# A two-block transformer-like layer at sequence 256: the residual and most products turned from feature-major to token-major

## The reference, cut to what matters

```python
x: (1, 256, 2048) float32                      # T = 256 tokens, D = 2048 features
h    = rmsnorm(x, norm_mix_pre)
proj = h @ w_in                                # 2048 x 5120: pool input, q, f, i, g
mix  = concat(pool_mixer(...), hgrn2_mixer(...)) @ w_out
x    = x + rmsnorm(mix, norm_mix_post)
h    = rmsnorm(x, norm_mlp_pre)
x    = x + rmsnorm(square(relu(h @ w_mlp_in)) @ w_mlp_out, norm_mlp_post)   # 8192 hidden
m    = silu(c) @ ada_w + ada_b                 # six vectors of 2048, one row c
n    = rmsnorm(x, norm_g[0]) * (1 + m[1]) + m[0]
z    = gelu(n @ a_w_in); u, v = split(z)       # 4096 each
s    = w_s . rmsnorm(v) (+ b_s)                # mixing over tokens in chunks of 128
x    = x + m[2] * ((u * s) @ a_w_out)
n    = rmsnorm(x, norm_g[1]) * (1 + m[4]) + m[3]
z    = conv3 along tokens of (n @ ffn_w_up); g, v = split(z)                # 5632 each
x    = x + m[5] * ((silu(g) * v) @ ffn_w_down)
out  = rmsnorm(x, final_g)
```

## Time and profile before

| | us |
|---|---|
| median of 3 runs (range) | 2573.86 (2572.02 to 2575.58) |
| span of the profiled execution | 2572.2 |
| PE busy in it | 2494.5 (97%) |
| DVE busy | 1682.6 (65%) |
| ACT busy | 1154.8 (45%) |

### The profile page before, as it was taken

One profiled execution on the slowest core, in us unless ns is written; L12 is line 12 of the kernel. 1 busy time (PEld: TensorE's weight loads), 2 busy tenths in 40 slices (PEclk: granted clock), 3 DMA queues, 4 the chain that ended last, 5 costly groups with the idle time before them and its releaser, 6 DMA issues.

```text
span 2572.2 us, 50625 instructions
## 1 busy us (share of the span) xinstructions
PE 2494.5 (97%) x19544; PEld 2437.4 (95%) x19544; DVE 1682.6 (65%) x1941; ACT 1154.8 (45%) x1344; POOL 100.1 (4%) x71
## 2 busy tenths in 40 slices
PE   8999998999999999998999999998999999999998
PEld 7989997999999999997888999998999999999997
DVE  6784767776675765776866876655666556655665
ACT  5554544543543543543544533434544344443443
POOL 0330011000000000001000000000000000000000
PEclk9999998999999999998999999999999999999999
DMA  6434453776777776774787776454555555555553
GB/s 224 140 132 164 141 194 109 299 274 253 260 278 254 257 278 251 257 273 168 262 312 259 271 279 237 158 187 151 184 180 174 194 173 181 182 184 180 187 181 123
DMA packets 151486, 542.88 MB, mean 211 GB/s; under 512 B 17712, under 2 KB 20016, under 8 KB 151216
## 3 DMA queue, kind: packets, MB, share of 16 engines
q1 hardware_dynamic: 151344, 540.81, 59.8%
HBM read 538.64 MB, written 2.10 MB: 210 GB/s over the span
## 4 chain that ended last, share of the span: by engine, by line
PE 92%; DVE 4%; issue 2%; ACT 1%; DMA 1%; POOL 0%; DVEq 0%; SPq 0%; ACTq 0%
PE bank L340 28%; PE bank L341 27%; PE bank L342 27%; PE bank L356 2%; PE bank L357 2%; PE bank L358 2%; PE mis L420 1%; DVE acc L1022 1%; DMA raw<-wstream 1%; DVE wlo L969 1%; PE mis L524 1%; DVE rstd L1015 0%; PE bank L377 0%; PE mis L401 0%; ACT whi L575 0%
## 5 line engine op out<-in xcount | busy, mean ns | idle before, releaser
L969 DVE TENSOR_TENSOR wlo<-raw,whi 128x1024 fp32r<-128x1024 f32 x824 | 1011.1, 1236 | 717.2 <-ACT whi L575 712.7
L575 ACT ACTIVATE whi<-raw 128x1024 fp32r<-128x1024 f32 x824 | 861.3, 1056 | 1093.8 <-PE bank L342 794.2
L340 PE MATMUL bank<-xs,whi 128*128 128x256 f32 x3456 | 986.9, 286 | 33.1 <-issue 13.1
L341 PE MATMUL bank<-xs,whi 128*128 128x256 f32 x3456 | 983.4, 285 | 0.0
L342 PE MATMUL bank<-xs,wlo 128*128 128x256 f32 x3456 | 983.3, 285 | 0.0
L340 PE MATMUL bank<-hs,whi 128*128 128x256 f32 x2496 | 707.8, 284 | 0.0
L341 PE MATMUL bank<-hs,whi 128*128 128x256 f32 x2496 | 706.3, 283 | 0.0
L342 PE MATMUL bank<-hs,wlo 128*128 128x256 f32 x2496 | 706.3, 283 | 0.0
L340 PEld LDWEIGHTS bank<-xs,whi 128*128 128x128 f32 x3456 | 669.4, 194 | 36.0 <-issue 28.7
L341 PEld LDWEIGHTS bank<-xs,whi 128*128 128x128 f32 x3456 | 669.4, 194 | 0.3 <-issue 0.2
L342 PEld LDWEIGHTS bank<-xs,wlo 128*128 128x128 f32 x3456 | 669.0, 194 | 0.0
(11 more groups left out here) (153 smaller groups left out, 1058.9 us busy)
## 6 DMA issues: line engine op xcount, KB each, us to landing
raw<-wstream SPq DMA_DIRECT2D x824, 512.0 KB, 4.4
aring<-astream SPq DMA_DIRECT2D x192, 512.0 KB, 4.6
x<-xT SPq DMA_DIRECT2D x4, 512.0 KB, 5.6
outT<-acc SPq DMA_DIRECT2D x4, 512.0 KB, 2.7
pw<-poolw SPq DMA_DIRECT2D x1, 1024.0 KB, 9.2
ws<-wsT SPq DMA_DIRECT2D x8, 128.0 KB, 4.2
bs<-bsp SPq DMA_DIRECT2D x8, 128.0 KB, 4.6
mk<-masks SPq DMA_DIRECT2D x1, 288.0 KB, 8.5
```

The costliest lines, as they stand in the source:

```text
L340: pe.matmul(o, whi[:, slot, c], h, start=st, stop=False, skip_group_check=True)
L341: pe.matmul(o, whi[:, slot, c], l, start=False, stop=False, skip_group_check=True)
L575: act.activation(whi[:, slot, :], raw[:, slot, :], ACT.Copy).then_inc(hi_ready, 1)
L969: dve.tensor_tensor(wlo[:, slot, :], raw[:, slot, :], whi[:, slot, :].bitcast(F32), ALU.subtract).then_inc(lo_ready, 1)
```

## The change

The residual `x`, the accumulator `acc` and the outputs of most products become token-major (tokens on partitions). `token_unit` is now used for groups 4, 5, 8 to 69 and for all down groups of the feed-forward; `feature_unit` stays in groups 0 to 3, 6, 7 and in the feed-forward's up groups, where the convolution runs along tokens. Sums of squares run along the free axis, as an accumulated output of ACT's Square, so a norm's scale is one number to a partition. What a product takes as its stationary operand still needs features on partitions: PE transposes each 128x128 tile through the identity (`to_features` for a sublayer's input, eight steps of four transposes, three before its first unit and five between its units; `hidden_to_features` for a group of hidden activations, eight transposes between units of the next group; `heads_to_features` for the mixer). ACT and DVE make high and low parts from the transposed tiles in PSUM. Gains that multiply columns of a token-major tile are loaded as rows broadcast to all partitions, 1 MB each. Two of the six modulation vectors are now reduced by matmuls with a matrix of ones (`ada_row`), so that they come out broadcast. All `Fori` loops are written out.

```diff
@@ TensorE @@
+            def token_unit(src, kt0, n, first, last, pb):
+                pe.wait_ge(lo_ready, n + 1)
+                slot = n % RING
+                for k in range(UK):
+                    c = slice(k * NC, (k + 1) * NC)
+                    for b in range(2):
+                        o = bank[pb + b][:, :]
+                        h = src[:, kt0 + k, b * P:(b + 1) * P]
+                        l = src[:, kt0 + k, T + b * P:T + (b + 1) * P]
+                        pe.matmul(o, h, whi[:, slot, c], start=first and k == 0, stop=False)
...
+            def to_features(z, i):
+
+                pe.wait_ge(xn_ready, 8 * z + i + 1)
+                if i >= 4:
+                    pe.wait_ge(tm_ready, 8 * z + i - 3)
+                for k in range(2):
+                    for b in range(2):
+                        o = mis[i % 4][:, k * T + b * P:k * T + (b + 1) * P]
...
+            def hidden_to_features(hg, pair):
+                pe.wait_ge(tok_ready, hg + 1)
+                for m in range(MT):
+                    for b in range(2):
+                        mm = pe.transpose(mis[pair + m // 2][:, (m % 2) * T + b * P:(m % 2) * T + (b + 1) * P],
+                                          t1[:, b, m * P:(m + 1) * P], eye[:, :])
...
+            def ada_row(v):
+                pe.wait_ge(ada_used, (v + 1) * ADA_PER_VEC)
+                for c in range(4):
+                    mm = pe.matmul(mis[c][:, :], ones[:, :], aacc[:, c * NC:(c + 1) * NC], start=True, stop=True)
+                mm.then_inc(ada_sum, 2)
...
-            with pe.Fori(0, 4) as q:
-                with pe.Fori(0, 2) as p:
-                    for a in range(2):
-                        group(q * 8 + p * 2 + (G_MLP + a), xs, 2 * a, wait=xs0(1))
...
+            for q in range(4):
+                for p in range(4):
+                    j, hg = G_MLP + 8 * q + p, 4 * q + p
...
+            pe.wait_ge(ws_arrived, 16 * 8)
+            pe.wait_ge(ada_read, 5)
@@ ScalarE @@
+            def feature_tmp(z, i):
+                act.wait_ge(xt_done, 8 * z + i + 1)
...
+            def features(z, j, first=None):
+
+                feature_tmp(z, 0)
+                for i in range(8):
+                    if i < 7:
+                        feature_tmp(z, i + 1)
+                    act.wait_ge(tm_ready, 8 * z + i + 1)
+                    act.activation(xs[:, 2 * i:2 * i + 2, 0:T], tiles(t1[:, i % 2, :]), ACT.Copy).then_inc(xs_hi, 1)
...
+                def evac(j=j):
+                    if j >= 8:
+                        act.wait_ge(h_ff, 2)
+                        act.wait_ge(unit_used, evac_at(j))
+                        for b in range(2):
+                            act.activation(sgt[:, b, (j - 8) * NC:(j - 7) * NC], bank[2 * (j % 2) + b][:, :],
+                                           ACT.Sigmoid).then_inc(bank_free, 1)
@@ VectorE @@
+            def gate_take(v, gate, r):
+                dve.wait_ge(row_arrived[r], 16)
+                dve.wait_ge(ada_sum, 2 * v + 2)
+                for c in range(4):
+                    o = gate[:, c * NC:(c + 1) * NC]
+                    ins = dve.tensor_tensor(o, mis[c][:, :], o, ALU.add)
+                ins.then_inc(ada_read, 1)
...
+            def joined(i):
+                if i % 2 == 0:
+                    normed_sum(S_MIX, i * T, NC).then_inc(xn_ready, 2)
...
+            for g in range(8):
+                body(G_AV + g, None, after=(lambda i: gate_take(4, gate2, ROW_GATE) if i == 7 else None) if g == 7 else None,
+                     done=RING if g == 0 else 0)
```

More of the change, by code:

```diff
@@ L272, in ada @@
                     sp.wait_ge(ada_used, k - 1)
[L273 to L282, removed]
+                sp.dma_start(aring[:, k % 2, :], astream[k:k + 1, :, :].rearrange("o p w -> p (o w)")
+                             ).then_inc(ada_arrived[k % 2], 16)
@@ L359, in token_unit, with group @@
                 mm.then_inc(unit_used, 1)
[L361 to L365, removed]
+            def group(j, src, token=True, wait=None, between=None):
+                n, units = first_unit(j), units_of(j)
+                if j >= 2:
+                    pe.wait_ge(bank_free, 2 * j - 2)
@@ new lines, in _, with between @@
+                for g in range(4):
+                    def between(u, g=g):
+                        if g == 0 and u == 2:
+                            pe.wait_ge(hid_lo, 2 * (H_A + 4 * half + 3))
+                            hidden_to_features(H_A + 4 * half + 3, 2)
+                        if half == 0 and g == 3 and u == 6:
+                            ada_row(5)
+                    group(G_AU + 8 * half + 4 + g, hs, wait=lambda u: (hid_lo, 2 * (H_A + 4 * half) + u + 1),
+                          between=between)
@@ L561, in _ @@
+            enter(3)
+            for c in range(3):
+                ups = 8 if c < 2 else 6
+                for p in range(ups):
+                    group(G_FF + 12 * c + p, xs, token=False, wait=normed(3),
+                          between=entering(3) if c == 0 and p == 0 else None)
+                for g in range(4):
+                    group(G_FF + 12 * c + ups + g, hs, wait=lambda u: (hid_lo, 2 * (H_F + 4 * c) + u + 1))
         @block.scalar
         def _(act):
-            step = Count(act_step)
+            steps, cells, squares = [0], [0], [0]
@@ L575, in split, with body @@
                 act.activation(whi[:, slot, :], raw[:, slot, :], ACT.Copy).then_inc(hi_ready, 1)
[L577 to L580 removed]
+            def body(j, evac, after=None, done=0, last=True):
+                units = units_of(j)
                 for i in range(units):
[L582 removed]
+                    if i == units - 1 and evac:
@@ L837, in _ @@
-            mlp_quarter(0, early=True)
-            with act.Fori(1, 3) as q, step.loop(q, 2, 8, start=1):
-                mlp_quarter(q)
-            mlp_quarter(3, last=True)
-            root(3)
-            squares(4, x, ready=lambda i: sum_ready(1, i))
-            root(4)
-            split_xs(2, shift=mod[:, 0, :], meanwhile=early_splits(G_AV))
-            def gated_values(p, early=False):
-                for a in range(2):
-                    j = p * 2 + (G_AV + a)
-                    body(j * GU, lambda: gelu_v(j, p * 2 + a, a), done=0 if a or not early else EARLY)
@@ L1354, in _ @@
-            mlp_quarter(0, early=True)
-            ada_take(0)
-            with dve.Fori(1, 3) as q, step.loop(q, 2, 1, start=1):
-                mlp_quarter(q)
-                ada_take(q)
-            mlp_quarter(3)
-            dve.wait_ge(ada_read, 3)
-            link(dve.scalar_tensor_tensor(out=geff[:, :], in0=mod[:, 1, :], scalar=1.0, in1=gain[:, 4, :],
-                                          op0=ALU.add, op1=ALU.mult))
-            root(3)
-            normed_into_x(1, 3)
-            root(4)
@@ L1428, in _ @@
-            ffn_chunk(0, early=True)
-            ffn_chunk(1)
-            with dve.Fori(0, 3) as p, step.loop(p, 3, 4):
-                j = p * 2 + G_FT
-                body(j * GU, lambda: gate(j, 0, p + 8), late=True)
-                body((j + 1) * GU, lambda: value(j + 1, 1, p + 8, p + (H_F + 8), p * 4), late=True)
-            for g in range(4):
-                n = G_DT * GU + g * DTU
-                body(n, lambda: gated_into_x(n + DTU, g % 2, 4 * g, 5), units=DTU, s0=2 * (g % 2))
-            root(6)
```

1540 lines of the change are left out of this document (816 added, 724 removed).

## The result

| | median us | range | to the kernel before |
|---|---|---|---|
| before, timed beside it (4 runs) | 2574.15 | 2572.02 to 2575.58 | |
| after (4 runs) | 3398.55 | 3397.41 to 3401.96 | 1.3203 [1.3184, 1.3222] |

What follows compares the result with a forecast made beforehand. The prediction took PE, dense inside groups, as the bound, so the number and width of its instructions count. Its terms summed to -87.7 us, span 2572.2 to 2484.5, giving a median of 2486 us, range 2464 to 2513.

Steps and rivals of the forecast that it cites:

- DMA: Loads of the 1 MB gain rows, one as groups 46 and 47 start: between 0 and 6 us, 3.5 taken.
- Modulation: Reducing modulation vectors: two by `ada_row` matmuls, +3.5 us, and 1 us where `ada_columns` waits for the last tile.
- DMA becomes the bound: Rival: weight supply stays at its old pace in the MLP's 32 groups, 41 us given back, 2527 us; chance 0.08.
- Products: 520 units become token-major with half as many matmuls, 2.72 us a unit instead of 2.88: -83.2 us.
- Transposes: 0.85 us per eight in 24 MLP and chunk-mixer groups, +20.4 us; twenty at each of four entries, +8.6 us.
- Loops: Writing out loops removes PE's stops at three quarter turns and, at half, one of the feed-forward's chunks: -21.3 us.
- slower than before: Rival: reading the written-out program costs stops everywhere, 0.85 us in each of 104 groups using up the gain; chance 0.03.
- Boundaries: PE's stops: mixer to MLP 8.6 us (-17.2), MLP to chunk mixer 18 (-8), chunk mixer to feed-forward 9.2 (-0.6).
- New wait before group 54: PE stands while DVE reads the reduced vector behind group 53's last split, low clock after: +8.7 us, bounds 3 and 12.
- The start: Kernel start: first product at 17.2 us instead of 20.7, -3.5 us.
- The gains' row: 1 MB rows of gains, one asked for as groups 46 and 47 start: 3.5 us taken for all.
- Mixer's end and the kernel's end: Mixer's end, groups 8 to 10, head norms replaced and late splits: net +3.3 us; kernel's end 12.8 us for 15.7: -2.9.

Runs made afterwards that it cites:

- experiment 1: The changed kernel with SyncE asking for each modulation tile k where the kernel before did, instead of tile k+2 there: 2489.77 us, ratio 0.9665.
- experiment 6: Experiment 1 with each transpose of the hidden activations issued twice: 2510.21 us, ratio 0.9753.
- experiment 3: The kernel before with its loops written out and nothing else changed: 2551.32 us, ratio 0.9909.
- experiment 8: Experiment 7 with the fourth weight split placed behind the norm's root at the MLP's end, on ACT and DVE: 2474.57 us, ratio 0.9614.
- experiment 2: Experiment 1 with DVE reading the gate's vector ahead of the last weight split of group 53: 2478.58 us, ratio 0.9631.
- experiment 7: Experiment 2 with the gate's row and first part of the v gain asked for four groups later: 2478.11 us, ratio 0.9630.

## Why the prediction was wrong

**The step that failed** is in the parts "DMA" and "Modulation": the first prices only the gains' rows, the second only the reduction by `ada_row` and `ada_columns`. That the requests of the 192 modulation tiles stand at other places in SyncE's queue was left out, and with it a term of +909 us (experiment 1 against after). The account of the change shows lines of PE, ACT and DVE and none of SyncE, where this one stands. No rival held it: "DMA becomes the bound" is a want of bandwidth, and names "ACT waiting for DMA with PE waiting for it" as its sign. That sign did appear, 1428 us of it, with the DMA engines at 0.42. The same wait row can mean a full pipe or an empty one; the share beside it decides.

The price could have been worked out from the trace before: 4.4 us from request to landing, ACT 1.06 and DVE 1.24 and 1.28, 0.4 for the tile's request ahead of the unit's: 8.4 us in all, for a unit that PE needs every 2.72. These two lines of the page before were the missing ones (queue, count, size, us to landing):

```profile
raw<-wstream SPq DMA_DIRECT2D x824, 512.0 KB, 4.4
aring<-astream SPq DMA_DIRECT2D x192, 512.0 KB, 4.6
```

**The other terms,** which experiment 1 lays bare (2489.8 us for a forecast of 2486):

- *Products:* right. The group without transposes takes 21.77 us for 21.8, 0.2268 us a product of 512 columns, 13 ns over the 213.3 of its columns. The Trainium skill (TensorE: Matmul & The Clock Gate, "Wait — 56ns, not 53.3ns?") has 2.5 ns there for matmuls one behind the other; here each has a weight load of its own (13408 of both on the page after), and no row comes near it.
- *Transposes:* right, 0.85 us a set forecast and 0.85 by experiment 6 (0.88 in the unit that holds them). They were never late.
- *Loops:* right, 21.3 forecast and 23.1 by experiment 3. Writing out brought no stops of its own, so the rival "slower than before" had the right sign by the wrong mechanism.
- *Boundaries:* stops of 8.7, 19.7 and 9.4 us in experiment 1 for 8.6, 18 and 9.2. The first and third were right; the second was 1.7 too small, and experiment 8 shows that a split on its path is worth 2.1. (For the third the sum has -0.6, while its own numbers, 10.1 and 9.2, give -0.9.)
- *New wait before group 54:* right in kind, 9.9 us with its low clock for 8.7 (experiment 2).
- *The start:* the gain was put too high. The first product came at 19.37 us in experiment 1, for 17.2 forecast and 20.70 before.
- *The gains' row:* 3.5 forecast; it cost 5.1 us in group 47 (7.05 less 1.97, experiment 7), of which the whole time kept nothing when it was moved.
- *Mixer's end and the kernel's end:* read from the traces alone. Groups 8 to 10 took 79.8 us in experiment 1 for 79.4 before, with 3.8 us less of products: +4.2 for +3.3. From the last product on it was 13.3 us for 15.8: -2.5 for -2.9.

Experiment 1 lies 3.8 us over the forecast. The terms above are off by up to 2.2 us each, most of them upward, and the loops' 1.8 us the other way; so the nearness of the sum is a little better than its terms.

## What to carry to other kernels

When one queue carries requests for two rings, a request's wait belongs to everything behind it. Count for each request which unit must be finished before it goes out, and compare (time of one turn from request to release) / (units allowed under way) with the time that the consumer takes for one; here 8.4/3 = 2.8 was near enough to 2.72, and 8.4/1 cost 32%. Asking earlier is no gain in a queue that is in order, if the slot comes free only later; and a diff must be read on the issuing engine too, down to the number that a wait carries.

## What was unexpected of the hardware

The granted clock after a stop isn't set by the stop's length alone: behind the same 15.0 us of idle time, 2.79 us of twelve transposes and another 1.61 us of idle time, group 46's first unit took 3.19 us in experiment 2 and 5.45 in experiment 7. It isn't the edit either: experiment 1 has the same program on PE up to there and took 5.07. So it differs between executions of what PE sees as one program, and a gain of a few us should be read from the stretch where it is made as well as from the whole time.

The low clock of the changed kernel (0.876 on the mean, 0.79 and 0.77 in the stretches above) is a consequence, not the cause. Behind the stop of experiment 1 twelve matmuls at the low clock are 0.43 us apart, 5.1 us for a unit, and one turn of 8.4 us leaves room for them; and with the requests in turn the granted clock of the same kernel is 0.987.
